# The last feed-forward chunk in token thirds, with down products and layer-norm statistics ahead of its end

## Chip, cores and metric

The kernel runs on one core of a Trainium2 chip. The metric is the device time of one execution in microseconds (us), lower is better. A core has a matrix engine (TensorE, PE in the profile; PEld is its weight load), a vector engine (VectorE, DVE), an activation engine (ScalarE, ACT), GpSimd (POOL) and a queue engine that issues transfers (SyncE, SP). Each runs its own instructions in order; semaphores order them among each other.

## The reference

One step of a transformer layer over 1024 prompt tokens and 8 x 16 sample tokens (1152 tokens, width 1024). Only the end matters here, the convolutional feed-forward layer and the per-layer embedding:

```python
up = x1 @ w_up                                   # 1024 -> 2 x 2816
ext = concatenate([conv_prev, up], axis=1)
conv = conv_b + sum(conv_w[j] * ext[:, j:j + T] for j in range(3))
val, gate = split(conv, 2, axis=-1)
ffn = (val * gelu(gate)) @ w_down                # 2816 -> 1024
x2 = layer_norm(ALPHA * x1 + ffn, ln2_g, ln2_b)
e = (p @ w_pl) * sigmoid(x2 @ w_plg)
y = layer_norm(ALPHA * x2 + e, ln3_g, ln3_b)
```

The last two columns of `ext` of each sequence (`conv_new`) are an output too. Everything is float32; each product is made of three products of rounded halves (`hi*hi`, `hi*lo`, `lo*hi`, `split3`), so that each operand needs a `hi` copy (ACT) and a `lo` subtraction (DVE or POOL).

## The kernel before

**Chunks.** The 2816 hidden columns are 22 chunks of 128 (`NC_FF`; `LAST` = 21). Chunk d has six *up thirds* `up(j, d, v, g)`: v = 0 the value half, v = 1 the gate half, g one of three token thirds of 384 (`THIRD`), 24 matmuls each. ACT copies each third from PSUM into `U` (line 1569). DVE convolves a whole half in three dependent steps over 1168 columns (`convolve`, lines 2123 to 2127), ACT applies gelu (1589), DVE multiplies (2168), ACT makes `hh` (1593) and DVE `hl` (2173, 2174). A chunk's down product has 18 *half-tiles* (9 token tiles of 128 times two halves of 512 columns), three matmuls each; `down` (1049) makes them on PE in the *next* chunk, between its up thirds by the list `DOWN_AFTER` (395): 0 to 4 after the third up product, 5 to 10 after the fourth, 11 to 17 after the fifth. They rotate through three PSUM banks: half-tile w waits until `add_down` on DVE (2134) has added half-tile w - 3 into `x1`.

**The last chunk.** Its up thirds come in the order (v,g) = 00, 01, 02, 10, 11, 12, the down half-tiles of chunk 20 between them. Before the sixth, `turn_p_early` (1062) transposes three tiles of the embedding input p. Its own down product comes behind the chunk as whole tiles, `last_down(n)` (1110). In between `embed_p(0..2)` (1100) makes p @ w_pl for tiles 0 to 2.

**The end.** For each of nine token tiles: `add_last` (DVE, 2198), `second_a` (statistics and centring, line 2044 ff.), `row_rstd` on POOL (two small operations, 2429 and 2431, in the order of the statistics), `second_b` (scaling, giving x2; `scale`), `turn_x2` (PE transposes, 1122), `x2_hi` (ACT), `x2_lo` (DVE, 2211), `gate(n)` (PE, x2 @ w_plg in two halves of 24 matmuls, 1140), sigmoid (ACT), `third_a` and `third_b` (DVE), store. The weights `w_plg` come in eight blocks k: SP loads them once the last up product is made (2690), ACT makes `plg_hi(k)` (1544), and `plg_lo(k)` is made by DVE for k = 0, 1, 7 (2138) and by POOL for k = 2 to 6 (2476). The first half of `gate(0)` waits for each block k in turn (1134 to 1138). The layer-norm gains and biases g2, b2, g3, b3 are broadcast by SP after block 1.

**What sets the order.** All of it is written out by hand: the order in each engine's block is the order of execution. Products behind the chunks take four PSUM slots in rotation (`take`, 342); a taker waits until the product four back is drained. POOL's order behind the chunks is plg_lo(2), plg_lo(3), row_rstd (tile 0), store of the last new columns (`store_new`), plg_lo(4), row_rstd (tile 1), plg_lo(5), plg_lo(6), and then all other row_rstd. DVE's is plg_lo(1), add_last(0), second_a(0), add_last(1), second_b(0), second_a(1), add_last(2), add_last(3), x2_lo(0), second_b(1), plg_lo(7), add_last(4), add_last(5), and then the loop over tiles, whose first step is second_a(2).

Of the kernel before, what the change touches and what calls it, by code (L numbers as in the profile page):

```python
# [88 lines left out]
def build(nc, x_prompt, x_sample, cache_fox_k, cache_fox_v, cache_fox_logf, state_gla, cache_ffn_conv,  # L89
# [4 lines left out]
    with ctx:  # L94
# [294 lines left out]
        def up_use(j, d, v, g):  # L389

            n = 6 * d + 3 * v + g
            return n % 4, 3 * j + n // 4
# [215 lines left out]
        def _(pe):  # L608
# [453 lines left out]
            def turn_p_early():  # L1062
                for v, g in ((0, 2), (1, 0)):
                    b, n = up_use(0, LAST, v, g)
# [20 lines left out]

            def chunk(j, d):
                if d == 0:
                    first_chunk()
                    return
                for g in range(6):  # L1090
                    if d == LAST and g == 5:
                        turn_p_early()
# [66 lines left out]
            pe.wait_ge(s_hl, NC_FF)  # L1159
            pe.wait_ge(s_dl, NC_FF)  # L1160
            for n in range(4):
                last_down(n)
            turn_x2(0)
# [20 lines left out]
        def _(act):  # L1184
# [371 lines left out]
            def halves(j, d):  # L1556

                more = d != NC_FF - 1
                for v in range(2):
                    act.wait_ge(s_cg, 4 * j + 2 * d + v + 1)  # L1560
                    u = U[:, v, :]
                    for g in range(3):
                        b, n = up_use(j, d, v, g)
                        act.wait_ge(up_full[b], n + 1)
                        if d == LAST and v == 1 and g == 2:
                            o = product(act, "pTs")
                            copy(pTh, o[:, 0:768].rearrange("p (n k t) -> p n k t", n=3, k=2)).then_inc(s_x2h, 1)
# [6 lines left out]
                    if v == 0:  # L1574
                        if more:
                            up_hi(j, d + 1, 0)
                            up_hi(j, d + 1, 1)
# [19 lines left out]
            in_pairs(act, halves)  # L1597
            keep_p(1)
            plg_hi(1)
            keep_p(2)  # L1600
            plg_hi(2)
            act.wait_ge(s_ocn, 32 * LAST)
            o = product(act, "columns")
            copy(cno, o[0:18, 0:256]).then_inc(drained("columns"), 1)
            for k in range(3, KT - 1):
                plg_hi(k)
# [10 lines left out]

            x2_hi(0)
            plg_hi(KT - 1)
# [15 lines left out]
        def _(dve):  # L1635
# [504 lines left out]
            def halves(j, d):  # L2140
# [598 lines left out]
```

## Time and profile before

| | us |
|---|---|
| median of 3 runs | 2348.92 (2347.63 to 2351.49) |
| profiled execution | 2349.89 |
| its span, first to last instruction | 2348.2 |
| PE busy | 2288.3 (97%) |
| DVE busy | 1280.9 (55%) |
| ACT busy | 675.3 (29%) |
| POOL busy | 269.1 (11%) |

The chunks fill most of the execution with PE busy throughout. The last chunk's up products run from about 2136.7 to 2175.2 us of the span, the first half of gate(0) from 2206.26 to 2211.84, and PE's last matmul ends near 2333.6. A row of the timeline gives start and duration of an instruction, or of several merged ones (x2), and in brackets how long the engine was idle before it and who released it. Matmuls overlap, so their starts, not their durations, give PE's pace.

### The profile page before, as it was taken

How to read it: one execution, taken by the hardware profiler on the slowest of the kernel's cores; microseconds unless marked ns; L12 is line 12 of the kernel's file. 1: busy time of each engine (PE TensorE's matmuls, PEld its weight loads, DVE VectorE, ACT ScalarE, POOL GpSimd, SP SyncE). 2: the span in 40 equal slices, each digit the busy share in tenths (PEclk: the TensorE clock that was granted, in tenths of full speed). 3: DMA queues.
4: the chain of work that ended last, by engine and by line, in shares of the span. 5: the costliest groups of instructions: out<-in, count | busy, mean ns of one | idle time of the engine just before them, and what ended most of it. 6: DMA issues, size and time to landing. Idle time of an engine off the chain costs nothing.

```text
span 2348.2 us, 31921 instructions
## 1 busy us (share of the span) xinstructions
PE 2288.3 (97%) x13055; PEld 2116.7 (90%) x13055; DVE 1280.9 (55%) x1696; ACT 675.3 (29%) x1100; POOL 269.1 (11%) x462
## 2 busy tenths in 40 slices
PE   8999999999999999999999999999999999999897
PEld 8997777898989899999998899999999999999686
DVE  2226753363636363112433666667676766767885
ACT  3124663333333332123221231222212122221310
POOL 0001222001010101000031210000000000000331
PEclk9999999999999999999999999999999999999998
DMA  5109654112120212213215011111101111111310
GB/s 159 42 24 253 165 153 127 52 28 85 29 84 21 86 28 79 80 46 104 59 63 170 1 46 46 37 45 36 54 27 54 45 36 45 36 45 35 115 52 36
DMA packets 154750, 160.27 MB, mean 68 GB/s; under 512 B 14538, under 2 KB 127158, under 8 KB 153990
## 3 DMA queue, kind: packets, MB, share of 16 engines
q1 hardware_dynamic: 145638, 128.91, 18.5%
q0 software_dynamic: 9008, 29.87, 4.0%
q8 instruction: 78, 1.28, 0.2%
q14 instruction: 26, 0.21, 0.0%
HBM read 122.27 MB, written 23.84 MB: 62 GB/s over the span
## 4 chain that ended last, share of the span: by engine, by line
PE 91%; DVE 3%; SPq 2%; issue 1%; ACT 1%; DMA 1%; POOL 0%; DVEq 0%; ACTq 0%; POOLq 0%
PE ps L613 73%; PE ps L1140 4%; PE ps L1019 3%; PE ps L930 2%; PE ps L793 1%; DVE sb L1645 1%; SPq L2572 1%; PE ps L645 1%; PE ps L775 1%; PE ps L753 1%; DVE sb L1749 0%; PE ps L981 0%; PE ps L776 0%; PE ps L960 0%; DMA kc<-k_lo 0%
## 5 line engine op out<-in xcount | busy, mean ns | idle before, releaser
L613 PE MATMUL ps<-x_hi,up_hi 128*128 128x384 f32 x1056 | 353.8, 335 | 0.1
L613 PE MATMUL ps<-x_hi,up_lo 128*128 128x384 f32 x1056 | 353.7, 335 | 0.0
L613 PE MATMUL ps<-x_lo,up_hi 128*128 128x384 f32 x1056 | 353.2, 334 | 0.0
L1194 ACT ACTIVATE sb<-ps 128x384 f32<-128x384 f32 (+5 forms) x332 | 132.5, 427 | 716.7 <-PE ps L613 664.2
L613 PE MATMUL ps<-x_hi,ring_hi 128*128 128x384 f32 x960 | 328.2, 342 | 3.4 <-DVE x_lo L1669 2.6
L613 PE MATMUL ps<-x_hi,ring_lo 128*128 128x384 f32 x960 | 322.4, 336 | 0.0
L613 PE MATMUL ps<-x_lo,ring_hi 128*128 128x384 f32 x960 | 322.4, 336 | 0.0
L2134 DVE TENSOR_TENSOR sb<-sb,ps 128x512 f32<-128x512 f32 x378 | 258.5, 688 | 114.1 <-PE ps L613 113.7
L613 PEld LDWEIGHTS ps<-x_hi,up_hi 128*128 128x128 f32 x1056 | 198.2, 188 | 2.7 <-DVE sb L1645 0.3
L613 PEld LDWEIGHTS ps<-x_lo,up_hi 128*128 128x128 f32 x1056 | 198.2, 188 | 2.4
L613 PEld LDWEIGHTS ps<-x_hi,up_lo 128*128 128x128 f32 x1056 | 198.2, 188 | 0.0
L1659 DVE TENSOR_TENSOR ring_lo<-ring_raw,ring_hi 128x1024 fp32r<-128x1024 f32 (+1 forms) x66 | 75.9, 1156 | 207.9 <-ACT ring_hi L1194 207.3
L613 PEld LDWEIGHTS ps<-x_hi,ring_hi 128*128 128x128 f32 x960 | 181.5, 189 | 7.3 <-issue 7.0
L613 PEld LDWEIGHTS ps<-x_lo,ring_hi 128*128 128x128 f32 x960 | 181.7, 189 | 1.0 <-issue 0.7
L613 PEld LDWEIGHTS ps<-x_hi,ring_lo 128*128 128x128 f32 x960 | 181.4, 189 | 0.0
L613 PE MATMUL ps<-down_hi,h_hi 128*128 128x512 f32 x396 | 156.9, 396 | 0.8 <-DVE h_lo L2174 0.7
L613 PE MATMUL ps<-down_hi,h_lo 128*128 128x512 f32 x396 | 155.4, 392 | 0.0
L613 PE MATMUL ps<-down_lo,h_hi 128*128 128x512 f32 x396 | 155.1, 392 | 0.0
L1645 DVE SCALAR_TENSOR_TENSOR convolved_halves<-sb,convolved_halves 128x1168 f32<-128x1168 f32 x88 | 126.3, 1435 | 11.1 <-DVE convolved_halves L2123 1.4
L1645 DVE SCALAR_TENSOR_TENSOR sb<-sb 128x1024 f32<-128x1024 f32 (+4 forms) x78 | 94.0, 1221 | 31.1 <-ACT sb L1410 24.4
L613 PE MATMUL ps<-ring_hi,x_hi 128*128 128x256 f32 x360 | 104.7, 291 | 0.0
L613 PE MATMUL ps<-sb 128*128 128x256 f32 (+4 forms) x400 | 101.8, 391 | 0.1
(280 smaller groups left out, 4243.3 us busy)
## 6 DMA issues: line engine op xcount, KB each, us to landing
ring_raw<-in_w_in SPq DMA_DIRECT2D x50, 512.0 KB, 3.9
up_raw<-in_w_up SPq DMA_DIRECT2D x44, 512.0 KB, 3.9
sb<-in_x_prompt SPq DMA_DIRECT2D x24, 512.0 KB, 8.3
down_raw<-in_w_down SPq DMA_DIRECT2D x22, 512.0 KB, 4.5
branch_b<-sb POOLq DMA_DIRECT2D x4, 1152.0 KB, 7.2
ob_raw<-branch_b POOLq DMA_DIRECT2D x3, 1536.0 KB, 7.4
kk<-k_hi SPq DMA_DIRECT2D x16, 256.0 KB, 4.3
sb<-in_cache_fox_k SPq DMA_DIRECT2D x8, 512.0 KB, 6.7
```

The source lines that it names most:

```text
L613: m = mm(out, l, r, start=(n == 0), stop=(n == len(pairs) - 1))
L645: m = tr(o[:, k * P:(k + 1) * P], x[:, k * P:(k + 1) * P], ident)
L753: mm(o, qq[:, t], kk[:, a:b], start=True, stop=False)
L775: mm(o, kk[:, k], qq[:, a:b], start=True, stop=False)
L793: m = mm(o, v[:, j, :], p[:, x], start=(j == n == 0), stop=(j == 4 * c + 3 and n == 2), skip_group_check=True)
L930: m = mm(o[:, t], a[:, t], c[:, t], start=True, stop=True)
L1019: m = mm(o[:, 0:512], a, b, start=(k == i == 0), stop=(k == KT - 1 and i == 2))
L1140: m = mm(o, a, b, start=(k == i == 0), stop=(k == KT - 1 and i == 2))
L1194: return act.activation(out, in_, ACT.Copy, scale=scale)
L1645: return dve.scalar_tensor_tensor(out=out, in0=in0, scalar=scalar, in1=in1, op0=op0, op1=op1)
L1659: dve.tensor_tensor(ringl[:, i, 0:kt], ring[:, i, 0:kt], ringh[:, i, 0:kt].bitcast(F32), ALU.subtract)\
L2134: dve.tensor_tensor(z, z, bank[:, 4 + b, :], ALU.add).then_inc(dn_free[b], 1)
```

## The change

The last chunk gets code of its own on PE, ACT and DVE; all other chunks stay.

- **PE.** The up thirds of chunk 21 come in pairs of one token third (order 00, 10, 01, 11, 02, 12; `up_use` numbers their banks so). The half-tiles of chunk 20 keep their places, after the third, fourth and fifth up product. After the fifth come `turn_p_early`, the half-tiles 0 to 3 (tiles 0 and 1) of chunk 21 itself, the sixth up product, and half-tiles 4 and 5 (tile 2). Behind the chunk: embed_p(0), embed_p(1), last_down(3), turn_x2(0), embed_p(2), columns, last_down(4), last_down(5), gate(0).
- **ACT and DVE** copy, convolve, gelu, multiply and split by thirds (0 to 384, 384 to 768, 768 to 1168 columns). On DVE: two convolution thirds, adds 0 to 4, h third 0, wdl, the pll splits, two convolution thirds, adds 5 to 10, h third 1, adds 11 to 17, p_lo, adds 0 to 3 of chunk 21, statistics of tiles 0 and 1, adds 4 and 5, two convolution thirds; then centring of tile 0, h third 2 and so on.
- **POOL** gathers the new columns of chunk 21 only after all of its convolutions, makes the row_rstd of tiles 0 and 1 inside the chunk, and then plg_lo(2), store_new, plg_lo(3), row_rstd (now of tile 2), plg_lo(4), (5), (6).
- **SP** loads g2 and b2 ahead of the eight blocks of w_plg, g3 and b3 behind them.

```diff
         def up_use(j, d, v, g):
-            n = 6 * d + 3 * v + g
+            n = 6 * d + (2 * g + v if d == NC_FF - 1 else 3 * v + g)
...
+            def last_chunk():
+                up(0, LAST, 0, 0)
+                up(0, LAST, 1, 0)
+                up(0, LAST, 0, 1)
+                new_columns(0, LAST - 1)
+                down(0, LAST - 1, DOWN_AFTER[2])
+                up(0, LAST, 1, 1)
+                down(0, LAST - 1, DOWN_AFTER[3])
+                up(0, LAST, 0, 2)
+                down(0, LAST - 1, DOWN_AFTER[4])
+                turn_p_early()
+                down(0, LAST, range(4))
+                up(0, LAST, 1, 2)
+                down(0, LAST, range(4, 6))
...
-                pe.wait_ge(dn_free[b], 6 * LAST)
+                pe.wait_ge(dn_free[b], 6 * LAST + 2)
             embed_p(1)
-            pe.wait_ge(dn_free[2], 6 * LAST)
+            pe.wait_ge(dn_free[2], 6 * LAST + 2)
             pe.wait_ge(cn_free, LAST)
+            last_down(3)
+            turn_x2(0)
             embed_p(2)
...
-            for n in range(4):
-                last_down(n)
-            turn_x2(0)
             last_down(4)
             last_down(5)
...
+            def last_thirds():
+                dve.wait_ge(s_hl, LAST)
+                convolve_third(0, 0)
+                convolve_third(1, 0)
+                add_down(0, LAST - 1, DOWN_AFTER[2])
+                h_third(0)
...
+                h_lo_third(0)
+                for k in range(2):
+                    dve.wait_ge(s_plh, k + 1)
+                    dve.tensor_tensor(pll[:, k, :], rpl[:, k, :], plh[:, k, :].bitcast(F32), ALU.subtract).then_inc(s_pl, 1)
+                convolve_third(0, 1)
+                convolve_third(1, 1)
+                add_down(0, LAST - 1, DOWN_AFTER[3])
+                h_third(1)
+                h_lo_third(1)
+                add_down(0, LAST - 1, DOWN_AFTER[4])
+                dve.wait_ge(s_x2h, 1)
...
+                add_down(0, LAST, range(4))
+                for n in range(2):
+                    tile_added(n)
+                    second_i[n] = stats_of(x1[:, n, :])
+                add_down(0, LAST, range(4, 6))
+                convolve_third(0, 2)
+                convolve_third(1, 2)
...
+            dve.wait_ge(s_g1, 64)
+            centre(x1[:, 0, :], second_i[0], g2)
+            h_third(2)
+            second_b(0)
+            h_lo_third(2)
+            plg_lo(0)
+            add_last(3)
+            centre(x1[:, 1, :], second_i[1], g2)
             plg_lo(1)
...
+            second_b(1)
             x2_lo(0)
...
             add_last(4)
             add_last(5)
+            plg_lo(KT - 1)
+            dve.wait_ge(s_const, 48)
...
                 if d:
                     store_new(j, d - 1)
+                if d == LAST:
+                    row_rstd()
+                    row_rstd()
                 gather(j, d, 0)
...
             plg_lo(2)
+            copied(pool, "columns")
+            store_new(0, LAST, columns_copied=True)
             plg_lo(3)
             row_rstd()
-            copied(pool, "columns")
-            store_new(0, LAST, columns_copied=True)
             plg_lo(4)
-            row_rstd()
             plg_lo(5)
             plg_lo(6)
...
+            bcast(ln2_g[0], g2, s_g1)
+            bcast(ln2_b[0], b2, s_g1)
             for k in range(KT):
                 sp.dma_start(rplg[:, k, :], w_plg[0, k * P:(k + 1) * P, :]).then_inc(s_xt[k], 16)
...
+            bcast(ln3_g[0], g3, s_const)
+            bcast(ln3_b[0], b3, s_const)
```

## Rows read from the trace of the kernel before

**Rows 1.** Waits of PE from 2130 us: total, times, longest

```profile
PE ps L1122 <- DVE sb L1645: 7.7, 1, 7.7
PE ps L613 <- DVE p_lo L2164: 2.1, 1, 2.1
PE ps L613 <- DVE h_lo L2174: 0.7, 1, 0.7
PE ps L1140 <- DVE x_lo L2211: 0.6, 1, 0.6
```

**Rows 2.** Windows: us, busy of PE, PEld, DVE, ACT, POOL, PEclk, DMA, GB/s

```profile
2192.40:2200.10 7.70, 0.00 (x0) 0.00 (x1) 7.70 (x4) 1.03 (x1) 6.47 (x6) 0.74 0.23 76
2200.10:2203.00 2.90, 2.90 (x11) 2.71 (x12) 2.83 (x5) 0.89 (x1) 1.34 (x2) 0.51 0.00 0
2211.84:2333.70 121.86, 121.75 (x575) 101.19 (x573) 96.20 (x112) 20.03 (x25) 33.54 (x30) 1.00 0.10 38
```

**Rows 3.** Timeline of PE: start, duration, engine, line, operation

```profile
2152.88 0.33 PE L613 MATMUL ps<-x_hi,up_hi 128*128 128x384 f32 x1
...
2157.07 0.39 PE L613 MATMUL ps<-down_hi,h_hi 128*128 128x512 f32 x1
...
2161.19 0.33 PE L613 MATMUL ps<-x_hi,up_hi 128*128 128x384 f32 x1
...
2200.10 1.97 PE L1122 MATMUL ps<-sb 128*128 128x128 f32 x8 [7.72 <-DVE sb L1645]
...
2203.07 0.40 PE L613 MATMUL ps<-down_hi,h_hi 128*128 128x512 f32 x1
...
2211.84 1.04 PE L1122 MATMUL ps<-sb 128*128 128x128 f32 x8
```

**Rows 4.** Timeline of DVE behind the last chunk

```profile
2189.64 1.29 DVE L2044 BATCH_NORM_STATS2 sb<-sb 128x6 f32<-128x512 f32 x2
...
2191.21 3.52 DVE L1645 SCALAR_TENSOR_TENSOR sb<-sb 128x1024 f32<-128x1024 f32 x1
...
2195.78 4.27 DVE L1645 SCALAR_TENSOR_TENSOR sb<-sb 128x1024 f32<-128x1024 f32 x1
...
2201.52 1.28 DVE L1645 SCALAR_TENSOR_TENSOR sb<-sb 128x1024 f32<-128x1024 f32 x1
```

**Rows 5.** Timeline of POOL behind the last chunk

```profile
2188.89 4.74 POOL L2476 TENSOR_TENSOR plg_lo<-plg_raw,plg_hi 128x1024 fp32r<-128x1024 f32 x2 [7.72 <-ACT plg_hi L1194]
...
2195.42 1.16 POOL L2462 DMA_DIRECT2D out<-sb  x2
2196.59 2.36 POOL L2476 TENSOR_TENSOR plg_lo<-plg_raw,plg_hi 128x1024 fp32r<-128x1024 f32 x1
2201.58 1.31 POOL L2429 TENSOR_SCALAR sb<-sb 128x1 f32<-128x1 f32 x1 [2.62 <-DVE sb L2046]
2202.97 0.57 POOL L2431 TENSOR_TENSOR sb<-sb 128x1 f32<-128x1 f32 x1
```

**Rows 6.** Timeline of DVE in the last two chunks

```profile
2137.69 0.89 DVE L2123 TENSOR_SCALAR convolved_halves<-sb 128x1168 f32<-128x1168 f32 x1 [3.12 <-ACT sb L1194]
2138.61 2.91 DVE L1645 SCALAR_TENSOR_TENSOR convolved_halves<-sb,convolved_halves 128x1168 f32<-128x1168 f32 x2
...
2150.40 3.37 DVE L2134 TENSOR_TENSOR sb<-sb,ps 128x512 f32<-128x512 f32 x5 [3.50 <-PE ps L613]
...
2157.96 4.11 DVE L2134 TENSOR_TENSOR sb<-sb,ps 128x512 f32<-128x512 f32 x6 [0.45 <-PE ps L613]
```

**Rows 7.** Groups by form: busy, mean ns of one, idle before (whole span; ACT 2180 to 2200)

```profile
L2156 DVE TENSOR_TENSOR down_lo<-down_raw,down_hi 128x1024 fp32r<-128x1024 f32 x22 | 26.8, 1219 | 0.0
...
L2017 DVE TENSOR_TENSOR merged_lo<-gate_a,merged_hi 128x384 fp32r<-128x384 f32 x24 | 13.2, 548 | 0.0
...
L1194 ACT ACTIVATE plg_hi<-plg_raw 128x1024 fp32r<-128x1024 f32 x7 | 7.3, 1050 | 0.3 <-DMA plg_raw<-in_w_plg 0.2
```

**Rows 8.** DMA issues from 2174 us: size, median us to landing

```profile
sb<-in_ln_b SPq DMA_DIRECT2D x2, 512.0 KB, 7.6
```

More of the change, by code:

```diff
@@ L1062, in turn_p_early @@
             def turn_p_early():
-                for v, g in ((0, 2), (1, 0)):
-                    b, n = up_use(0, LAST, v, g)
+                for v in range(2):
+                    b, n = up_use(0, LAST, v, 1)
                     pe.wait_ge(up_free[b], n + 1)
@@ L1595, in halves, with halves_or_last @@
                      y[:, 0, SEQ + 2:SEQ + 146].rearrange("p (b t) -> p b t", t=18)[:, :, 0:DEC_T]).then_inc(s_hh, 1)
[L1597 to L1606, printed above, removed]
+            def halves_or_last(j, d):
+                if d == LAST:
+                    last_thirds()
+                else:
+                    halves(j, d)
@@ L1616, in x2_hi @@
                     copy(pTh[:, n % 3], o[:, 0:256].rearrange("p (k t) -> p k t", k=2)).then_inc(s_x2h, 1)
+            keep_p(0)
+            plg_hi(0)
+            keep_p(1)
+            plg_hi(1)
             x2_hi(0)
-            plg_hi(KT - 1)
+            keep_p(2)
+            plg_hi(2)
+            act.wait_ge(s_ocn, 32 * LAST)
+            o = product(act, "columns")
+            copy(cno, o[0:18, 0:256]).then_inc(drained("columns"), 1)
+            for k in range(3, KT):
+                plg_hi(k)
             for n in range(NT):
@@ L2175, in halves, with convolve_third @@
                                   rows(hh[:, e, SEQ:T].bitcast(F32), DEC_B, DEC_T), ALU.subtract).then_inc(s_hl, 1)
-            dve.wait_ge(s_xa, NT)
-            in_pairs(dve, halves)
+            def convolve_third(v, g):
+                n, (a, b) = 2 * LAST + 2 * g + v + 1, Y_THIRDS[g]
+                i, m = up_use(0, LAST, v, g)
+                dve.wait_ge(up_free[i], m + 1)
+                if g == 2:
+                    dve.wait_ge(s_up, 2 * LAST + v + 1)
+                u, yv = U[:, v, :], y[:, v, a:b]
+                w = [cwT[:, c, LAST + v * NC_FF:LAST + v * NC_FF + 1] for c in range(4)]
+                dve.tensor_scalar(yv, u[:, a:b], w[0], w[3], ALU.mult, ALU.add).then_inc(s_cv1, 1)
+                dve.wait_ge(s_cv1, n)
+                stt(yv, u[:, a + 1:b + 1], w[1], yv, ALU.mult, ALU.add).then_inc(s_cv2, 1)
+                dve.wait_ge(s_cv2, n)
+                stt(yv, u[:, a + 2:b + 2], w[2], yv, ALU.mult, ALU.add).then_inc(s_conv, 1)
@@ new lines, in h_third, with h_lo_third @@
+            def h_third(g):
+                a, b = Y_THIRDS[g]
+                dve.wait_ge(s_gel, LAST + g + 1)
+                dve.tensor_tensor(y[:, 0, a:b], y[:, 0, a:b], y[:, 1, a:b], ALU.mult).then_inc(s_hm, 1)
+            def h_lo_third(g):
+                a, b = Y_THIRDS[g]
+                e = LAST % 2
+                dve.wait_ge(s_hh, LAST + g + 1)
+                if g < 2:
+                    dve.tensor_tensor(hl[:, e, a:b], y[:, 0, a:b], hh[:, e, a:b].bitcast(F32), ALU.subtract).then_inc(s_hl, 1)
+                    return
+                dve.tensor_tensor(hl[:, e, a:SEQ], y[:, 0, a:SEQ], hh[:, e, a:SEQ].bitcast(F32), ALU.subtract)
+                dve.tensor_tensor(rows(hl[:, e, SEQ:T], DEC_B, DEC_T), rows(y[:, 0, SEQ + 2:SEQ + 146], DEC_B, 18)[:, :, 0:DEC_T],
+                                  rows(hh[:, e, SEQ:T].bitcast(F32), DEC_B, DEC_T), ALU.subtract).then_inc(s_hl, 1)
@@ new lines, in tile_added, with last_thirds @@
+            def tile_added(n):
+                for w in (2 * n, 2 * n + 1):
+                    b, m = dn_use(0, LAST, w)
+                    dve.wait_ge(dn_free[b], m + 1)
+            def last_thirds():
+                dve.wait_ge(s_hl, LAST)
[3 more added lines that the diff above has]
+                h_third(0)
+                dve.wait_ge(s_dh, LAST + 1)
+                dve.tensor_tensor(wdl[:, LAST % 2, :], rawd[:, LAST % 2, :], wdh[:, LAST % 2, :].bitcast(F32), ALU.subtract)\
+                    .then_inc(s_dl, 1)
+                h_lo_third(0)
+                for k in range(2):
+                    dve.wait_ge(s_plh, k + 1)
[7 more added lines that the diff above has]
+                dve.wait_ge(s_x2h, 1)
+                o = product(dve, "pTs")
+                dve.tensor_tensor(pTl, o[:, 0:768].rearrange("p (n k t) -> p n k t", n=3, k=2), pTh.bitcast(F32),
+                                  ALU.subtract).then_inc(drained("pTs"), 1)
+                add_down(0, LAST, range(4))
[5 more added lines that the diff above has]
+                convolve_third(1, 2)
```

106 lines of the change are left out of this document (57 added, 49 removed).

## The prediction

> **What bounds the kernel now.** The text works on the profiled execution, 2349.89 us with a span of 2348.2; the median of the three runs is 0.97 us lower. I read four views. The waits of TensorE (PE) behind 2130 us come first: between the last up products and the gate products PE idles 7.7, 2.1, 0.7 and 0.6 us [rows 1], 11.1 us in all, which is nearly all that a reordering can win. The windows come second. From 2211.84 to 2333.70 PE is busy 121.75 of 121.86 us [rows 2], so everything behind the first half of gate(0) only follows PE; the diff leaves that loop alone. **The measure is therefore one number: when the first half of gate(0) ends, 2211.84 before** (turn_x2(1) starts there, [rows 3]). The same windows show PE's granted clock at 0.51, the 1.2 GHz level, from 2200.10 to 2203.00, after the idle stretch 2192.40 to 2200.10 (mean 0.74) [rows 2]. Third, the timelines of VectorE (DVE) and GpSimd (POOL) say what made the 7.7 us: scale(0) on DVE started at 2195.78 and took 4.27 us instead of 1.28, and ended 1.1 us after POOL's plg_lo(4) (2196.59 + 2.36); centre(0) took 3.52 and ended 1.1 us after POOL's second plg_lo (2188.89 + 4.74) [rows 4, 5]. A DVE operation with two SBUF inputs stands still while POOL runs a plg_lo. Fourth, the timeline of the last chunk gives the pace at which PE and DVE trade down products.
>
> **The durations used.** A convolution of one half takes 0.92 + 2.91 = 3.83 us for 1168 columns in three dependent steps [rows 6]. A subtraction is 1.22 us at 1024 and 0.55 at 384 columns [rows 7], 1.05 ns a column and 0.15 fixed; two multiply-adds go at that rate and the first tap (0.89 for 1168) at half of it, so a third of 384 costs 3.83 - 784 x (1.05 + 1.05 + 0.52) ns = 1.77 us, and the last of 400 columns 1.81; bounds 1.28 (a third of 3.83) and 2.1. A 1024-wide DVE step advances 1.15 us, statistics of one tile 1.55 (2189.64 to the next step at 2191.21, [rows 4]), a copy of 1024 on ScalarE (ACT) 0.95 (1.05 less the overlap with the next, [rows 7]). On PE an up third is 4.19 us (2152.88 to 2157.07) and six down half-tiles 4.12 (to 2161.19), so one is 0.69 [rows 3].
>
> **Part 1, thirds in the chunk.** PE's sum of work is unchanged. Until the first five adds end (2150.40 + 3.37 = 2153.77, [rows 6]) nothing is late: the first two convolution thirds fit into DVE's idle time ahead of them. But DVE now does h_third(0) 0.57, wdl 1.14, h_lo_third(0) 0.56, two pll 2.35 and two convolution thirds 3.54 *before* adds 5 to 10, which it started at 2157.96 [rows 6]. That is 8.16 us, to 2161.9. PE starts half-tile 5 at 2157.07 [rows 3] and has three banks, so half-tile 8 needs add 5. A fourth term comes from POOL: store_new(20) moves from a place beside adds (which read PSUM) to about 2155.6, beside pll. In the trace two such issues at 2195.42 took 1.16 us, and the DVE operation behind them did not get through before POOL's next one [rows 4, 5]. I charge 0.7 (bounds 0 and 1.16). Add 5 then ends at 2163.3 and PE, through with half-tile 7 at 2159.2, idles about 4.2 us that did not exist before. Half-tile 10 ends at 2165.5 instead of 2161.19 [rows 3].
> The Trainium skill ("SBUF — State Buffer", section "Who interferes with whom") says that a DVE operation with two SBUF inputs contends only with GpSimd work that reads SBUF, and infers that descriptor writing is not such work. By it the 0.7 is 0; [rows 4, 5] speak against it, since scale(0) was dispatched ahead of plg_lo(4) and still ended behind it.
>
> **Part 2, down products and statistics ahead of the end.** From 2165.5: up(0,2) 4.19, seven half-tiles 4.81, the turning of p 0.6 (six transposes, eight show 1.04 with their overlap, [rows 3]), to 2175.1; p_hi and p_lo, 768 columns wide, 0.8 and 0.95 with two hand-overs, to 2177.15; adds 0 to 3 2.7, to 2179.8; two statistics 3.1, to 2182.9. On PE half-tile 3 waits 0.4 for add 0, up(1,2) ends at 2182.7, half-tiles 4 and 5 at 2184.1; their adds end at 2185.0. The last two convolution thirds 3.6 (2188.6), centre(0) 1.25, h_third(2) 0.57, scale(0) 1.2: x2(0) is ready at 2191.6, against 2200.05 before. SP issues g2 and b2 when up(1,2) ends; a broadcast took 7.6 us with three and more transfers ahead [rows 8], the first two of the queue should take 4 to 5.5, landing by 2188.3, hidden by 0.3 us behind the convolution; if that cover is gone, each us late costs one. The two row_rstd of tiles 0 and 1 lie beside adds and cost nothing. So **the chain that the change attacks becomes 8.4 us shorter**; embed_p(0), embed_p(1) and last_down(3) fill PE until 2191.0.
>
> **Part 3, what is late next.** Behind x2(0): ACT ends the last hh at 2191.05, then keep_p(0), plg_hi(0), keep_p(1), plg_hi(1), x2_hi(0), keep_p(2), plg_hi(2), seven steps of 0.95: plg_hi(2) at 2197.8. DVE: h_lo 0.6, plg_lo(0) to 2194.2, add_last(3), centre(1), plg_lo(1), scale(1) to 2199.0, x2_lo(0) 2200.1. last_down(5) takes the PSUM slot of x2T(0), so it waits for x2_lo(0) and ends at 2201.55, its add at 2203.0. POOL runs plg_lo(2) behind scale(1), 2199.0 to 2201.4, the issues of store_new(21) 1.16, plg_lo(3) to 2204.9. DVE's plg_lo(7) has two SBUF inputs and stands until then: 2206.05. **Then the decisive wait:** POOL's next instruction is now the row_rstd of tile 2, whose statistics DVE only takes behind plg_lo(7), at 2206.05 + 1.55 = 2207.6. Queued behind it on POOL are plg_lo(4), (5), (6), and gate(0) on PE waits for each. Before, the row_rstd at that place belonged to tile 1, and POOL went at 2201.58, after 2.62 us of waiting [rows 5]. The row_rstd takes 1.31 + 0.08 + 0.57 [rows 5] and two hand-overs, to 2209.65; three plg_lo of 2.37 [rows 5] end at 2216.8; k = 6 and 7 on PE cost 1.4, to 2218.2. PE has idled 6.4 us ahead of k = 4 by then. After the 7.7 us idle the clock was at 0.51, and eight transposes took 1.97 instead of 1.04 [rows 2, 3]; up to 2203.07 that stretch cost 1.4 us over its later pace. I take these 1.4 again (bounds 0 and 1.5): 2219.6. The 1.4 of before go with the 7.7 and are no gain of their own, because POOL and not PE paces the new gate(0).
>
> **The sum.** 2219.6 - 2211.84 = +7.8 us: 2357.7 against 2349.89, and about 2357 against the median. Bounds: convolution thirds at 1.28 instead of 1.8 take 1.0 off the first stall and, by the four thirds, 2.0 in all; no hold by POOL's issue 0.7; no clock loss 1.4; together +3.7. Thirds at 2.1 add 1.2, the full hold 0.5, a clock loss also in the first stall 1.4: +10.9. The order of scale(1) and plg_lo(2) moves 0.6 either way.
>
> **Rivals.** (a) *The first stall is absent and POOL is not kept waiting:* DVE reaches the adds before PE needs them and tile 2's statistics before plg_lo(3) ends. Then all lies 4.2 us earlier, plg_lo(3) at 2200.7, three plg_lo to 2207.8, gate half at 2209.2, -2.6 us: 2346. It decides from statistics ahead of 2200.7; my walk has 2207.6. For it: the chain to x2(0) is really shorter. Against: 8.16 us of DVE work in front of add 5, all of it ordinary operations. (b) *The mechanism is right but short:* DVE's steps overlap better by 3 us or more and the clock stays: +1 to +4, 2350 to 2353. For it: adds follow each other every 0.67 [rows 6] where I took 0.7, 1024-wide steps overlap by 0.1, and some thirty steps stand in the walk, each of which I may have taken too long by that. (c) *The clock also falls in the first stall and b2 lands late:* +9.5 to +12, 2359 to 2361. Against: the 2.1 us idle of [rows 1] had no such price. (d) *The change does not do what it says:* x2(0) is not early because centre(0) waits for g2 and b2; +2 to +4 on top of the forecast, 2360.
>
> **How the numbers follow.** Forecast (2354 to 2359) 0.58, (a) 0.10, (b) 0.22, (c) 0.06, (d) 0.04. What a measurement of this kernel can tell from no change is about 0.2%, 4.7 us: slower begins at 2353.6. Faster by more than that needs more than all of (a), 0.05; within it the rest of (a) and nearly all of (b), 0.25; slower 0.70. The range 2349.5 to 2361 leaves out (a) and the far ends of (c) and (d).
>
> **What the profile after would show.** Step by step: a PE wait of about 4 us in the down products near 2159; turn_x2(0) near 2192; a PE wait of about 3 us ahead of last_down(5), for x2_lo; on POOL a row_rstd between plg_lo(3) and plg_lo(4) that waits for DVE's statistics; then three waits of PE inside gate(0) on POOL's plg_lo, about 6.4, 1.7 and 1.7 us, with a low granted clock there; from the end of that half on the same 136.4 us as before. Wrong would be: no wait of PE on plg_lo, or statistics of tile 2 ahead of 2201.

## The result, and the profile after

| | before | after |
|---|---|---|
| median, us (6 runs each) | 2350.51 (2347.63 to 2352.91) | 2359.53 (2357.66 to 2360.34) |
| profiled execution | 2349.89 | 2359.83 |
| its span | 2348.2 | 2358.1 |

The ratio of after to before over their runs is 1.0046, 95% interval 1.0036 to 1.0056 (the quotient of the two medians above, 9.0 us apart, is 1.0038): the change makes the kernel slower.

**A frame first.** In the profiled execution of after the convolution of chunk 20, untouched code, already starts at 2139.86, and at 2137.69 before [rows 6]: 2.17 us late. Such an offset is in each trace below (from -1.5 to +2.2 us, with identical code ahead), so steps are compared after taking it off, "in before's time". Of the 9.9 us between the two spans, 2.17 lie ahead of the change. The first half of gate(0) ends at 2221.41, which is 2219.24 in before's time against 2211.84 [rows 3]: **+7.40 us**. Behind it after takes 136.69 us to the end of its span and before 136.36: +0.33.

The waits of PE behind 2130 us, after (total, times, longest), answer to [rows 1]:

```profile
PE ps L1159 <- POOL plg_lo L2591: 8.1, 4, 5.9
PE ps L615 <- DVE sb L2180: 3.3, 2, 2.8
PE ps L615 <- DVE x_lo L2322: 3.0, 1, 3.0
PE ps L1141 <- DVE sb L1691: 0.7, 1, 0.7
```

The 7.7 us for x2(0) (turn_x2, now L1141) are down to 0.7. In their place stand 3.3 us on down adds, 3.0 on x2_lo(0) and 8.1 on POOL's plg_lo: 15.1 us instead of 11.1. The timeline of PE, the answer to [rows 3], gives their places:

```profile
2164.33 0.80 PE L615 MATMUL ps<-down_hi,h_hi 128*128 128x512 f32 x1 [2.85 <-DVE sb L2180]
...
2180.17 0.50 PE L615 MATMUL ps<-down_hi,h_hi 128*128 128x512 f32 x1 [0.42 <-DVE sb L2180]
...
2194.17 1.09 PE L1141 MATMUL ps<-sb 128*128 128x128 f32 x8 [0.68 <-DVE sb L1691]
...
2202.63 0.47 PE L615 MATMUL ps<-down_hi,h_hi 128*128 128x512 f32 x1 [2.98 <-DVE x_lo L2322]
...
2207.17 0.50 PE L1159 MATMUL ps<-plg_hi,x_hi 128*128 128x512 f32 x1 [0.87 <-POOL plg_lo L2591]
...
2214.06 0.79 PE L1159 MATMUL ps<-plg_hi,x_hi 128*128 128x512 f32 x1 [5.93 <-POOL plg_lo L2591]
...
2216.37 0.79 PE L1159 MATMUL ps<-plg_hi,x_hi 128*128 128x512 f32 x1 [0.67 <-POOL plg_lo L2591]
...
2218.69 0.79 PE L1159 MATMUL ps<-plg_hi,x_hi 128*128 128x512 f32 x1 [0.67 <-POOL plg_lo L2591]
...
2221.41 0.75 PE L1141 MATMUL ps<-sb 128*128 128x128 f32 x3
```

What made the 5.93 stands in POOL's timeline, against [rows 5]:

```profile
2200.14 3.45 POOL L2591 TENSOR_TENSOR plg_lo<-plg_raw,plg_hi 128x1024 fp32r<-128x1024 f32 x1 [8.83 <-ACT plg_hi L1210]
2203.54 1.16 POOL L2574 DMA_DIRECT2D out<-sb  x2
2204.72 2.39 POOL L2591 TENSOR_TENSOR plg_lo<-plg_raw,plg_hi 128x1024 fp32r<-128x1024 f32 x1
2209.74 1.31 POOL L2541 TENSOR_SCALAR sb<-sb 128x1 f32<-128x1 f32 x1 [2.62 <-DVE sb L2092]
2211.13 0.57 POOL L2543 TENSOR_TENSOR sb<-sb 128x1 f32<-128x1 f32 x1
2211.68 6.95 POOL L2591 TENSOR_TENSOR plg_lo<-plg_raw,plg_hi 128x1024 fp32r<-128x1024 f32 x3
```

and in DVE's, the answer to [rows 4] (plg_lo(7), the statistics of tile 2, and the next work):

```profile
2205.43 2.77 DVE L2184 TENSOR_TENSOR plg_lo<-plg_raw,plg_hi 128x1024 fp32r<-128x1024 f32 x1
2208.13 1.27 DVE L2090 BATCH_NORM_STATS2 sb<-sb 128x6 f32<-128x512 f32 x2
2209.43 0.21 DVE L2092 BATCH_NORM_AGGREGATE sb<-sb 128x2 f32<-128x12 f32 x1
2209.68 1.28 DVE L1691 SCALAR_TENSOR_TENSOR sb<-sb 128x1024 f32<-128x1024 f32 x1
2223.80 1.22 DVE L2322 TENSOR_TENSOR x_lo<-ps,x_hi 128x1024 fp32r<-128x1024 f32 x1 [12.84 <-ACT x_hi L1210]
```

POOL sits 2.62 us in front of the row_rstd of tile 2, spends 1.9 on it, and the last three blocks follow. Once DVE has made centre(2), it does nothing for 12.84 us, while POOL makes these blocks and PE waits for them and works them off. The windows, us and then busy time of PE, PEld, DVE, ACT, POOL, the granted clock, DMA share and GB/s, answer to [rows 2]:

```profile
2164.33:2167.88 3.55, 3.55 (x10) 2.87 (x10) 2.41 (x4) 0.00 (x0) 0.00 (x0) 0.58 0.00 0
...
2207.20:2214.06 6.86, 0.93 (x3) 0.45 (x4) 3.69 (x5) 0.00 (x0) 4.24 (x4) 0.83 0.00 0
2214.06:2221.41 7.35, 6.02 (x12) 3.70 (x13) 0.00 (x0) 0.00 (x0) 4.57 (x2) 0.50 0.00 0
```

The clock was at its lower level (0.50, 1.2 GHz) all through the stretch behind the 5.93 us, and for most of the stretch behind the first stall, whose mean is 0.58; in before the row that shows it lies behind the 7.7 us [rows 2].

### The profile page after: what moved, and what is told of

It is laid out like the page before. It is cut to its first block, busy times and chain, and to the rows that moved or that the text cites. A ratio compares the mean times of both kernels' runs of the same rounds, so it can differ in the third digit from the quotient of the medians.

```text
span 2358.1 us, 31950 instructions
## 1 busy us (share of the span) xinstructions
PE 2297.2 (97%) x13055; PEld 2122.6 (90%) x13055; DVE 1278.2 (54%) x1715; ACT 675.4 (29%) x1104; POOL 268.1 (11%) x462
## 3 DMA queue, kind: packets, MB, share of 16 engines
q8 instruction: 78, 1.28, 0.2%
## 4 chain that ended last, share of the span: by engine, by line
PE 91%; DVE 4%; ACT 1%; issue 1%; DMA 1%; POOL 1%; SPq 0%; DVEq 0%; ACTq 0%; POOLq 0%
PE ps L615 72%; PE ps L1159 4%; PE ps L1021 3%; PE ps L932 2%; PE ps L795 2%; PE ps L755 1%; PE ps L777 1%; PE ps L778 1%; DVE sb L1795 1%; PE ps L647 1%; DVE sb L1691 1%; PE ps L983 0%; PE ps L756 0%; PE ps L962 0%; PE ps L904 0%
## 5 line engine op out<-in xcount | busy, mean ns | idle before, releaser
L1691 DVE SCALAR_TENSOR_TENSOR convolved_halves<-sb,convolved_halves 128x1168 f32<-128x1168 f32 (+2 forms) x96 | 128.1, 1334 | 11.4 <-DVE convolved_halves L2169 1.2
L1691 DVE SCALAR_TENSOR_TENSOR sb<-sb 128x1024 f32<-128x1024 f32 (+4 forms) x78 | 87.0, 1132 | 31.3 <-ACT sb L1426 24.4
```

The lines of the kernel that those rows point to most:

```text
L1691: return dve.scalar_tensor_tensor(out=out, in0=in0, scalar=scalar, in1=in1, op0=op0, op1=op1)
```

## The experiments

Each was a variant of the changed kernel (labels a_) or of the kernel before (b_). "Gate end" is the end of the first half of gate(0) in before's time, to be held against 2211.84; ratios are against the kernel before, for the experiments on the same chip, with the 95% interval. The gate end is one profiled execution on each side, the ratio all runs.

| | gate end | ratio |
|---|---|---|
| changed kernel | 2219.2 | 1.0046 (1.0036 to 1.0056) |
| a_rstd_late | 2214.6 | 1.0021 (1.0011 to 1.0031) |
| a_adds_first | 2218.5 | 1.0042 (1.0029 to 1.0056) |
| a_both | 2213.4 | 1.0020 (1.0011 to 1.0029) |
| a_adds_idle | 2216.3 | 1.0026 (1.0016 to 1.0036) |
| a_dve | 2210.1 | 0.9998 (0.9989 to 1.0007) |
| a_full | 2206.0 | 0.9981 (0.9972 to 0.9990) |
| a_full2 | 2204.2 | 0.9975 (0.9966 to 0.9984) |
| b_pool | 2211.9 | 1.0011 (1.0002 to 1.0020) |
| b_port | 2212.4 | 1.0010 (1.0001 to 1.0020) |
| b_rstd2 | 2219.0 | 1.0041 (1.0027 to 1.0055) |
| b_dve | 2217.8 | 1.0021 (1.0012 to 1.0031) |
| b_dve2 | 2209.0 | 0.9996 (0.9987 to 1.0005) |

**a_rstd_late: the row_rstd of tile 2 behind the last plg_lo.**

```diff
             plg_lo(3)
-            row_rstd()
             plg_lo(4)
             plg_lo(5)
             plg_lo(6)
-            for n in range(2 * NT - 3):
+            for n in range(2 * NT - 2):
                 row_rstd()
```

> The changed kernel with one edit: POOL's row_rstd of tile 2 stands behind plg_lo(6) instead of ahead of plg_lo(4). Theory 1 (POOL's queue: the row_rstd waits for DVE's statistics of tile 2 and holds up the weights of gate(0)): plg_lo(4) starts right behind plg_lo(3), at about 2207.1 instead of 2211.7 us of the changed kernel's span, the three end at 2214.2 instead of 2218.6, the 5.9 us wait of PE falls to about 3, and the kernel is 4.4 to 5.8 us faster than the changed one, 3 to 5 slower than the kernel before (ratio 1.0015 to 1.002). Theory 2 (gate(0) would be late anyway, by the first stall in the chunk and by PE's clock): within 1 us of the changed kernel (ratio 1.004). Theory 3 (POOL back to back keeps DVE's plg_lo(7), with two SBUF inputs, out until plg_lo(6) ends): k = 7 waits about 1.2 us behind k = 6, and the gain is 3 to 4.5.

The gate end moves from 2219.2 to 2214.6, inside the 4.4 to 5.8 us of theory 1 (the ratio, 1.0021, is just past its 1.0015 to 1.002), and the first waits stay (2.85, 0.43, 0.67, 2.99 us). So the queued row_rstd is the larger part of the loss. What theory 3 foresaw for DVE came as well, though not its price in time:

```profile
2202.61 9.32 POOL L2591 TENSOR_TENSOR plg_lo<-plg_raw,plg_hi 128x1024 fp32r<-128x1024 f32 x4
...
2203.30 9.72 DVE L2184 TENSOR_TENSOR plg_lo<-plg_raw,plg_hi 128x1024 fp32r<-128x1024 f32 x1
```

DVE's plg_lo(7) stood through all four of POOL's and ended 1.1 us after the last. PE had no wait for it: POOL alone paces gate(0), one block in 2.33 us.

**b_rstd2: the same fault put into the kernel before,** tile 2's row_rstd ahead of plg_lo(5).

```diff
             row_rstd()
+            row_rstd()
             plg_lo(5)
             plg_lo(6)
-            for n in range(2 * NT - 2):
+            for n in range(2 * NT - 3):
                 row_rstd()
```

> The kernel before with one row_rstd moved on POOL: that of tile 2 stands ahead of plg_lo(5), as in the changed kernel it stands ahead of plg_lo(4). The mechanism alone, without thirds: POOL waits for DVE's statistics of tile 2, done near 2212.4, plg_lo(6) ends at 2219.1, k = 6 and 7 cost 1.4 to 2.8, the first half of gate(0) ends at 2220.5 to 2222 instead of 2211.8: 8.5 to 10 us slower, ratio 1.0036 to 1.0043, with a PE wait of about 6 us on plg_lo inside gate(0). If POOL's row_rstd has no hold over gate(0): no change.

The ratio came inside the forecast; the gate end, 2219.0, came ahead of the forecast 2220.5 to 2222. PE waits inside gate(0) as in the changed kernel, and POOL stands 8.77 us in front of the row_rstd of tile 2:

```profile
PE ps L1140 <- POOL plg_lo L2476: 7.3, 2, 6.7
PE ps L1122 <- DVE sb L1645: 4.6, 1, 4.6
...
2195.58 1.28 DVE L1645 SCALAR_TENSOR_TENSOR sb<-sb 128x1024 f32<-128x1024 f32 x1 [1.96 <-POOL sb L2431]
...
2209.68 1.31 POOL L2429 TENSOR_SCALAR sb<-sb 128x1 f32<-128x1 f32 x1 [8.77 <-DVE sb L2046]
```

In this execution x2(0) came 3.2 us earlier than before (4.6 of waiting for 7.7). The row at 2195.58 is scale(0): it started 0.2 us earlier than before and took 1.28 us instead of 4.27. (centre(0) took 1.28 us for 3.52 too, but that gain went into the 1.96 us that scale(0) then waited for the row_rstd.) gate(0) started at 2203.6 instead of 2206.3, and still its half ended 7.2 us late. The mechanism thus needs nothing else of the change: one row_rstd whose statistics stand behind plg_lo(7) in DVE's order, with plg_lo blocks queued behind it on POOL.

**a_adds_first and a_adds_idle: is the order on DVE the cause of the first stall?** Both take adds 5 to 10 ahead of pll and the second pair of convolution thirds. The first puts the two pll behind adds 11 to 17, ahead of p_lo:

```diff
                 h_lo_third(0)
-                for k in range(2):
-                    ... pll ...
+                add_down(0, LAST - 1, DOWN_AFTER[3])
                 convolve_third(0, 1)
                 convolve_third(1, 1)
-                add_down(0, LAST - 1, DOWN_AFTER[3])
                 h_third(1)
                 h_lo_third(1)
                 add_down(0, LAST - 1, DOWN_AFTER[4])
+                for k in range(2):
+                    ... pll ...
```

> The changed kernel with one edit on DVE: adds 5 to 10 of chunk 20 come right behind h_lo of the first third, ahead of the pll splits and of the two convolution thirds, and the pll splits come behind adds 11 to 17. Theory 1 (PE's first stall comes from DVE's order, and what follows is a chain that hangs on it): the 2.9 us wait and the low clock behind it (together 4.5 us) are replaced by a wait of 0.5 to 1.5 us for add 11, everything behind lies 3 to 4 us earlier, ratio to the kernel before 1.0022 to 1.0030 instead of 1.004. Theory 2 (only POOL's row_rstd matters and it is not moved by this): no change, 1.004.

A miss in the time: 1.0022 to 1.0030 was expected, and the ratio of 1.0042 can't be told from the changed kernel's. The 2.85 us stall is gone (up(0,2) starts at 2162.93), but p_lo and adds 0 to 3 now stand behind 2.35 us of pll, and half-tile 3 waits for them (timeline of PE, a_adds_first):

```profile
2177.73 0.50 PE L615 MATMUL ps<-down_hi,h_hi 128*128 128x512 f32 x1 [1.77 <-DVE sb L2180]
```

Behind that wait the clock is lower (windows, a_adds_first):

```profile
2177.73:2183.50 5.77, 5.77 (x23) 5.53 (x24) 4.60 (x9) 0.00 (x0) 1.53 (x4) 0.70 0.00 0
```

Of the 4.5 us by which up(0,2) starts earlier, 0.8 are left at the gate end.

a_adds_idle puts the two pll between the statistics of tile 1 and adds 4 and 5 instead, where DVE was idle 1.28 us:

```diff
-                for k in range(2):
-                    ... pll ...
+                add_down(0, LAST - 1, DOWN_AFTER[3])
                 convolve_third(0, 1)
                 convolve_third(1, 1)
-                add_down(0, LAST - 1, DOWN_AFTER[3])
...
                     second_i[n] = stats_of(x1[:, n, :])
+                for k in range(2):
+                    ... pll ...
                 add_down(0, LAST, range(4, 6))
```

> The changed kernel with adds 5 to 10 ahead of the two convolution thirds and the pll splits between the statistics of tile 1 and add 4 (the edit by which a_full differs from a_dve, on the changed kernel itself, POOL's order as changed). If the first stall costs 3.5 to 4.5 us of the changed kernel and a_adds_first lost it again only by the place of the pll splits, PE goes on at half-tile 8 without a wait, up(1,2) starts about 4.5 us earlier, and the kernel is 3 to 4.5 us faster than the changed one: ratio to the kernel before 1.0025 to 1.0035. If gate(0) is paced by something that this edit does not move: 1.004 to 1.005.

The ratio, 1.0026, came as expected; its interval touches the changed kernel's. In the trace it is 3.0 us at the gate end, all of them ahead of gate(0), with the four waits on plg_lo unchanged (8.1 us in all). The first stall is a matter of order. The stall and the low clock behind it took about 4.3 us; new waits of 0.8 us for an add and 0.65 for pl_lo take part of that back, so 3.0 us is what this order gains.

**a_both** has the two diffs of a_adds_first and a_rstd_late together.

> Both edits. If the two losses add up, as theory 1 has it, 7.5 to 9.5 us faster than the changed kernel, ratio to the kernel before 0.999 to 1.001. If they hide each other (the later one takes in the earlier), no better than the better of the two alone, about 1.0015.

Missed (0.999 to 1.001 was expected, 1.0020 measured) for the reason of a_adds_first: 1.78 us of waiting for adds in front of half-tile 3 take most of that part back. The gate end is 1.2 us ahead of a_rstd_late's, and the ratio is the same.

**b_pool and b_port: does POOL's DMA issue hold scale(0) on DVE?** In the kernel before scale(0) took 4.27 us, with POOL's issue of store_new and then plg_lo(4) beside it [rows 4, 5]. Both bring tile 0's row_rstd forward; b_pool has plg_lo(3) and (4) behind the issue, b_port the row_rstd of tile 1.

```diff
             plg_lo(2)
-            plg_lo(3)
             row_rstd()
             copied(pool, "columns")
             store_new(0, LAST, columns_copied=True)
+            plg_lo(3)
             plg_lo(4)
             row_rstd()
```

and for b_port, with plg_lo(3) taken from the same place:

```diff
             store_new(0, LAST, columns_copied=True)
-            plg_lo(4)
             row_rstd()
+            plg_lo(3)
+            plg_lo(4)
             plg_lo(5)
```

> The kernel before with one edit on POOL alone: plg_lo(2), row_rstd of tile 0, store_new, plg_lo(3), plg_lo(4), row_rstd of tile 1, plg_lo(5), plg_lo(6). Theory A (a DVE operation with two SBUF inputs waits for POOL's plg_lo but not for POOL's DMA issues): scale(0) starts near 2193.6 during the two DMA issues and takes 1.3 us, turn_x2(0) starts near 2195 instead of 2200.1, PE's 7.7 us wait falls to about 3, the clock stays up, and the kernel is 4 to 6 us faster, ratio 0.9975 to 0.9983. Theory B (DMA issues hold such an operation too, as I charged in the sum): scale(0) takes until the end of plg_lo(4) or plg_lo(3), about 2197 to 2200, and the gain is 0 to 3 us, ratio 0.9987 to 1.000.

> The kernel before with POOL's order plg_lo(2), row_rstd of tile 0, the two DMA issues of store_new, row_rstd of tile 1, plg_lo(3) to (6): behind the issues POOL has only a wait. Theory A (a DMA issue alone does not hold a DVE operation; in b_pool it was the plg_lo queued behind it): scale(0) starts near 2194 and takes 1.3 us. Theory B (the issue holds it): it takes until the issues end plus 1.1, about 1.9 us. Theory C (scale(0) is held by something else than POOL): 4 us and more, as before. Time: turn_x2(0) near 2195.5, then gate(0) waits for plg_lo(5) and (6), first half at about 2209.5 to 2211; 1 to 2.5 us faster, ratio 0.999 to 0.9997.

The rows of POOL and of scale(0), b_pool first:

```profile
2193.61 1.15 POOL L2462 DMA_DIRECT2D out<-sb  x2
2194.78 4.64 POOL L2476 TENSOR_TENSOR plg_lo<-plg_raw,plg_hi 128x1024 fp32r<-128x1024 f32 x2
...
2193.95 6.56 DVE L1645 SCALAR_TENSOR_TENSOR sb<-sb 128x1024 f32<-128x1024 f32 x1
```

and b_port:

```profile
2194.34 1.15 POOL L2462 DMA_DIRECT2D out<-sb  x2
2197.50 1.31 POOL L2429 TENSOR_SCALAR sb<-sb 128x1 f32<-128x1 f32 x1 [2.01 <-DVE sb L2046]
...
2194.69 1.28 DVE L1645 SCALAR_TENSOR_TENSOR sb<-sb 128x1024 f32<-128x1024 f32 x1
```

With the same issue running, scale(0) takes 1.28 us where only a waiting row_rstd stands behind the issue, and 6.56 where plg_lo does. So the issue doesn't hold DVE. A plg_lo right behind the issue can: in b_pool scale(0) was dispatched 0.83 us ahead of it and still ended after the second plg_lo, and 0.81 us ahead of it before [rows 4, 5]. It need not: in b_rstd2 scale(0), dispatched 1.10 us ahead of plg_lo(4) with the issue running, took 1.28. In time both missed: b_pool's 1.0011 lies above both of its theories, b_port's 1.0010 above the expected 0.999 to 0.9997. In b_pool PE waits 7.77 us for x2(0) as ever, in b_port only 2.52, but then 1.40 for add_last(3), and 1.65 and 2.34 inside gate(0), because plg_lo(3) to (6) come later. What DVE wins there, POOL's blocks lose: its four took 11.33 us. Why b_pool, with the gate end of before, is 2.6 us slower by its ratio, its trace doesn't show.

**a_dve, a_full, a_full2: POOL makes no plg_lo at all.** A block costs POOL 2.37 us [rows 5], and DVE's two-input work can stand still beside it (9.72 us for plg_lo(7) in a_rstd_late); DVE needs 1.15 for a block and was idle for 12.84. a_dve makes blocks 2 to 7 on DVE, behind x2_lo(0); a_full adds the order of a_adds_idle; a_full2 also puts x2_lo(0) ahead of plg_lo(1), and scale(1) behind all blocks. The edit of a_full2, without the part that it shares with a_adds_idle and the lists by which PE counts the blocks:

```diff
+            x2_lo(0)
+            for k in range(1, KT):
+                plg_lo(k)
-            plg_lo(1)
             second_b(1)
-            x2_lo(0)
             add_last(4)
             add_last(5)
-            plg_lo(KT - 1)
...
-            plg_lo(2)
             copied(pool, "columns")
             store_new(0, LAST, columns_copied=True)
-            plg_lo(3)
-            row_rstd()
-            plg_lo(4)
-            plg_lo(5)
-            plg_lo(6)
-            for n in range(2 * NT - 3):
+            for n in range(2 * NT - 2):
                 row_rstd()
```

> The changed kernel with all plg_lo on DVE: POOL makes none, DVE makes plg_lo(2) to (7) right behind x2_lo(0) and ahead of add_last(4). Theory 1 (the loss behind x2(0) is POOL's: 2.35 us a block, and DVE shut out while POOL runs): blocks 2 to 7 follow each other every 1.14 us from about 2200.3 (in a_rstd_late's time), the last is done at 2207.2, PE waits under 0.5 us for each block and its clock stays up, the first half of gate(0) ends at about 2207.9 against 2214.7 in a_rstd_late, 4 us ahead of the kernel before; ratio to the kernel before 0.998 to 0.9995. Theory 2 (six more operations on DVE, by then the engine in demand, only move the wait from POOL to DVE): first half of gate(0) at 2212 to 2214, or later waits in the loop on DVE's statistics of tiles 2 and 3; ratio 1.001 to 1.002.

> a_dve and adds 5 to 10 ahead of the two convolution thirds, with the pll splits this time between the statistics of tile 1 and add 4, where DVE idled 2.6 us in a_adds_first. Theory 1: the first stall (4.5 us with the low clock) is replaced by under 1 us for add 11, and nothing of it is eaten later, so 2 to 3.5 us faster than a_dve; ratio to the kernel before 0.997 to 0.9985. Theory 2 (as in a_adds_first the time comes back as another wait): within 1 us of a_dve.

> a_full with x2_lo(0) ahead of plg_lo(1) and scale(1) behind plg_lo(7). last_down(5) waits for x2_lo(0) 3.0 us; two DVE steps less ahead of it leave about 0.7 us, gate(0) starts 2.3 us earlier, plg_lo(7) is done one step earlier, and the first half of gate(0) ends 1 to 1.8 us earlier; turn_x2(1) then waits up to 1 us for scale(1). 0.5 to 1.8 us faster than a_full, ratio 0.9974 to 0.998. If the blocks from DVE pace gate(0) alone: nothing, 0.9981.

The three give 0.9998, 0.9981 and 0.9975; the last two came as expected and beat both kernels, by 1.9 to 2.5 thousandths of the time before. a_dve fell between its theories (0.998 to 0.9995, or 1.001 to 1.002). Its gate end came 2.3 us later than theory 1 has it: PE never waits for a block, but behind the 3.0 us wait for x2_lo(0) its granted clock was 0.50 until past 2207, in its own time. Since no row_rstd stands ahead of a plg_lo in these three, what the move to DVE itself brings is a_dve against a_rstd_late, not against the changed kernel: 1.0021 to 0.9998, and 4.5 us at the gate end. The waits of PE in a_full2:

```profile
PE ps L615 <- DVE sb L2180: 1.2, 2, 0.8
PE ps L615 <- DVE x_lo L2322: 0.7, 1, 0.7
PE ps L615 <- DVE pl_lo L2274: 0.6, 1, 0.6
PE ps L1159 <- DVE plg_lo L2184: 0.5, 3, 0.2
PE ps L1141 <- DVE sb L1691: 0.4, 2, 0.2
```

3.4 us in all, of 15.1 in the changed kernel. The seven blocks run as one row on DVE at 1.15 us each, with no plg_lo on POOL; POOL's issue of store_new (1.16 us from 2197.56) ran beside them and cost them nothing:

```profile
2197.03 8.02 DVE L2184 TENSOR_TENSOR plg_lo<-plg_raw,plg_hi 128x1024 fp32r<-128x1024 f32 x7
```

Of a_full to a_full2 the trace shows 1.8 us at the gate end (the wait for x2_lo(0) from 3.0 to 0.65, and no stretch at half clock behind it); the ratios differ by 0.0006, with overlapping intervals.

**b_dve and b_dve2: is that gain to be had without the thirds?** Both give the blocks to DVE in the kernel before; b_dve2:

```diff
             x2_lo(0)
+            for k in range(2, KT):
+                plg_lo(k)
             second_b(1)
-            plg_lo(KT - 1)
...
-            plg_lo(2)
-            plg_lo(3)
             row_rstd()
```

(and so for plg_lo(4) to (6) on POOL). b_dve put add_last(3) behind the blocks. That was an oversight in the experiment: gate(0) takes the PSUM slot that add_last(3) drains, and started only at 2210.3. b_dve2 has it back ahead of x2_lo(0).

> The kernel before with all plg_lo on DVE, blocks 2 to 7 behind x2_lo(0), add_last(3) and scale(1) behind them. If POOL's operations were what stretched centre(0) and scale(0) (together 5.2 us over their 1.3), turn_x2(0) starts near 2195 instead of 2200.1, the clock stays up, and the first half of gate(0) ends at about 2209.7 instead of 2211.8: 2 us faster, ratio 0.9985 to 0.9995. If the stretch has another cause, turn_x2(0) stays near 2200 and the kernel is 3 to 6 us slower, ratio 1.001 to 1.0025.

> b_dve with add_last(3) back ahead of x2_lo(0). In b_dve PE waited 7.5 us at gate(0), because its PSUM slot was that of last_down(3), drained by add_last(3), which stood behind six plg_lo: an oversight in that kernel. Now gate(0) should start near 2203 and its first half end at about 2211 in the time of the kernel before, if the granted clock stays up: ratio 0.9985 to 1.0005. It tells whether all plg_lo on DVE alone, without the token thirds, brings what a_full brings (0.998); I expect not, since the convolution, gelu and h chain of a whole half still lies ahead of x2(0).

b_dve shows what its mistake costs (1.0021), and one thing more: with no plg_lo on POOL, centre(0) and scale(0) take 1.28 us each, and PE waits 2.5 us for x2(0) instead of 7.7. b_dve2 is 0.9996 (0.9987 to 1.0005), no difference that can be measured from before, although its trace has the gate end 2.8 us early, x2(0)'s wait down to 2.5 us. Against it a_full2 stands at 0.9975 with intervals apart: the changed chunk and end as a whole are worth having once POOL makes no plg_lo. No run separates the thirds from the down products and statistics brought forward with them.

## Why the prediction was right, and where it was not

The forecast was 2357 us, range 2349.5 to 2361, slower at 0.70. Measured were 2359.53, slower, and inside the range, but above the 2354 to 2359 that had 0.58: the time lies where rival (c) was put (2359 to 2361, chance 0.06), and both things that (c) names happened, the clock fell in the first stall and b2 came late, by 0.25 us. Yet they aren't what lifts the time, since the walk itself came out as it was written, +7.7 us in the trace for +7.8. Its points, with measured times in before's time:

| step | predicted | measured |
|---|---|---|
| half-tile 10 ends | 2165.5 | 2165.7 |
| x2(0) ready (turn_x2(0) starts) | 2191.6 | 2192.0 |
| last_down(5)'s wait for x2_lo(0) | about 3 us | 2.98 us |
| statistics of tile 2 | 2207.6 | 2207.5 |
| its row_rstd ends | 2209.65 | 2209.5 |
| plg_lo(6) ends | 2216.8 | 2216.5 |
| half of gate(0) ends | 2219.6 | 2219.2 |

**Part 1, where the prediction failed: right in the sum by luck, wrong in its terms.** The new stall was charged at 4.2 us of waiting, of which 0.7 for POOL's issue beside pll, and no clock loss. Measured: a wait of 2.85 us, and then 3.55 us at a granted clock of 0.58, in which the last three half-tiles of the group take 1.5 us more than the 2.07 of three at 0.69. Together that is 4.3 us, so a wait charged about 1.3 us too long and a clock loss put at nothing cancel. Of the wait, the row of DVE work ahead of add 5 took 7.7 us (2153.8 to 2161.4 in before's time) where 8.16 was charged, and the issue cost nothing:

```profile
2157.89 1.07 POOL L2574 DMA_DIRECT2D out<-sb  x2 [13.52 <-ACT sb L1210]
...
2157.93 2.35 DVE L2260 TENSOR_TENSOR pl_lo<-pl_raw,pl_hi 128x1024 fp32r<-128x1024 f32 x2
```

The two pll take what two take alone (2.35 us in a_adds_first, with no issue beside them). One step that failed is the reading of [rows 4, 5], where scale(0) stood beside an issue *and* a plg_lo behind it, and the text gave the hold to the issue. b_port, b_pool and b_rstd2 separate the two. The Trainium skill ("SBUF — State Buffer", section "Who interferes with whom") had it right where the prediction weighed it and decided against it: writing descriptors is not work that a two-input DVE operation contends with. By the rule alone the wait would have been 3.5 us. The other step is the clock loss, placed in rival (c) with the 2.1 us wait of before as the reason against it. That one wait without a price did not show what a wait of 2.85 does: this one cost 1.5 us.

**Part 2, right.** Convolution thirds took 1.70 us (0.47 and 1.27 with the hand-over) where 1.77 was derived, bounds 1.28 and 2.1. The cover of 0.3 us for b2 was overrun by 0.25: centre(0) waited that long for the transfer. Rivals (c) and (d) had the mechanism, not the size.

**Part 3, right in mechanism, place and size.** What is off is the inner split of gate(0): predicted waits of 6.4, 1.7 and 1.7 us and 1.4 us of clock loss besides; measured 5.93, 0.67 and 0.67 (and 0.87 ahead of them, for plg_lo(3)), since each block of three matmuls takes 1.65 us at half clock instead of 0.69. As POOL paces the blocks, the slower PE only eats its own waits, except at the last ones. A clock loss under a pace set by another engine costs only behind the last hand-over: k = 6 and 7 took 2.7 us (2218.69 to 2221.41) for 1.4, so 1.3 was lost, as charged.

**What each part is worth on the chip.** Of the 7.4 us, the queued row_rstd makes 4.6 (a_rstd_late) and the first stall 3.0 (a_adds_idle). Their sum, 7.6, would bring the gate end level with before's if the two add up; they were not run together without the detour of a_both, so this is a sum and not a measurement. The 7.0 us by which x2(0)'s wait became shorter, and the 3.4 us of the other waits of before, went there: into 2.85 and 0.42 us on adds, 2.98 on x2_lo(0) and 8.1 on plg_lo.

**What stays open.** The medians differ by 9.0 us, the ratio of 1.0046 would be 10.8, and the walk holds 7.7. The other 1.3 to 3.1 us have no place; with them, and with a median of before that is 1.6 us higher over six runs than over the three of the forecast, the time came above 2357: the profiled execution shows 2.17 ahead of the change, but other kernels with the same code there show offsets from -1.5 to +2.1, with ratios that don't follow them. In every kernel of the table but b_dve the ratio makes it 1.3 to 3.4 us worse than its gate end does. All gate ends are held against one profiled execution of before, which may be the reason; no run shows it.

## What to carry to other kernels

When work is moved forward, look at what each engine's queue has next at the place it left: the row_rstd of tile 2 slid into the slot of tile 1, and a small operation with a late input held back 6.95 us of POOL work that was ready. Before splitting a batch of work between DVE and POOL, compare the price of one piece on each and look whether one holds up the other; here a piece took POOL 2.37 us and could block DVE meanwhile, DVE 1.15. Giving all of it to DVE took the ratio from 1.0021 (the row_rstd already out of the way) to 0.9998; with the DVE order mended as well it was 0.9975. Here a reordering that shortened one wait of 7.7 us earned nothing until the next limits, each a few microseconds behind, were moved too.

## What the runs showed of the hardware

**Whether a waiting DVE operation gets in between two POOL operations is not settled by its waiting.** DVE's plg_lo(7) stood 9.72 us through four plg_lo of POOL in a_rstd_late, and 8.62 in a_both. In b_port it was otherwise: POOL's four took 11.33 us, two of them 3.33, and DVE got in twice between them.

```profile
2199.45 11.33 POOL L2476 TENSOR_TENSOR plg_lo<-plg_raw,plg_hi 128x1024 fp32r<-128x1024 f32 x4
...
2202.04 3.23 DVE L1645 SCALAR_TENSOR_TENSOR sb<-sb 128x1024 f32<-128x1024 f32 x1
...
2205.19 3.37 DVE L2138 TENSOR_TENSOR plg_lo<-plg_raw,plg_hi 128x1024 fp32r<-128x1024 f32 x1
```

Even the same two instructions went either way: centre(0) at 2191.21 with POOL's pair begun at 2188.89 took 3.52 us before [rows 4, 5], and in b_rstd2, at 2191.20 with the pair begun at 2188.91, it took 1.28, and the pair 5.79 instead of 4.74. In the changed kernel POOL was the one that waited: plg_lo(2) took 3.45 us, with scale(1) dispatched 0.07 us ahead of it. What decides it the runs don't say.

**A wait of 2 to 3 us was followed by a lower granted clock in some places and not in others.** Behind a PE wait of 2.85 us it was 0.58 over the next 3.55 us; behind one of 2.98 us in the same execution it stayed at 1.00. Behind 1.77 us in a_adds_first it was 0.70 over 5.77 us. The same wait for x2_lo(0), 3.0 us, went both ways: in a_rstd_late and a_adds_idle the clock stayed at 1.00 over the next 3.4 us and more, in a_dve it was 0.50 over 4.6 us, and in a_full it was 0.53 over 3.5 us from 0.9 us behind its end. In a_rstd_late, where no wait inside gate(0) was over 1.35 us but PE was busy only 2.20 of 5.70 us, it fell to 0.50 behind that stretch too:

```profile
2203.90:2209.60 5.70, 2.20 (x8) 0.97 (x6) 5.70 (x1) 0.00 (x0) 5.70 (x4) 1.00 0.00 0
2209.60:2214.70 5.10, 4.37 (x9) 2.83 (x10) 5.03 (x5) 0.00 (x0) 2.48 (x3) 0.50 0.00 0
```
